# A planned transformer-block kernel on eight cores: gate pieces behind group 3's tiles, two more tile buffers, and new costs for GpSimd in the planner

## The reference

```python
mod_x = split(silu(c) @ w_ada + b_ada, 6)            # shift, scale, gate, twice
h   = layer_norm(x) * (1 + scale0) + shift0
q, k, v, u, vb, ga, gb = split(h @ w_in)
ya  = window_attention(rope(q), rope(k), v, kc, vc, sink)   # +-128 tokens and all context keys
yb  = gelu(u) * (w_s @ LN(gelu(vb)) + b_s)                  # per chunk of 128 tokens
mix = (sigmoid(ga) * (ya @ w_a) + sigmoid(gb) * (yb @ w_b)) @ w_out
x1  = post_norm(x, gate0 * mix)
h2  = layer_norm(x1) * (1 + scale1) + shift1
out = post_norm(x1, gate1 * ((silu(h2 @ w_g) * (h2 @ w_u)) @ w_d))
```

## Time and profile before

| | us |
|---|---|
| median of 3 runs | 981.92 |
| lowest and highest | 981.34, 982.61 |
| the profiled execution, its own time | 983.19 |
| its span from first to last instruction (core 4) | 981.4 |
| spans of the eight cores | 975.6 to 981.4 |
| PE busy / DVE / ACT / POOL | 897.0 / 624.9 / 321.6 / 275.3 |

### The profile page before, as it was taken

The page is one execution under the profiler, slowest core; times in us unless marked ns, Lnnn a source line. Parts: engine busy times, 40 slices in busy tenths (PEclk is TensorE's granted clock), DMA queues, the critical chain, the costliest instruction groups (busy, mean ns, idle before and its releaser), DMA issues.

```text
span 981.4 us, 15835 instructions; the slowest of 8 cores (975.6 to 981.4 us)
## 1 busy us (share of the span) xinstructions
PE 897.0 (91%) x5589; PEld 445.7 (45%) x5589; DVE 624.9 (64%) x1130; ACT 321.6 (33%) x497; POOL 275.3 (28%) x234
## 2 busy tenths in 40 slices
PE   1299697898999999999999999999999999999992
PEld 1245444344555444444444444444444444444761
DVE  5336687756655566776687575566556674666667
ACT  1336675546877243334435101110111001111101
POOL 6024164465464223323311630210202011000004
PEclk9999798989999999999999999999999999999997
DMA  8997621449972500027322580403304020111112
GB/s 211 195 196 179 166 87 44 108 55 167 146 106 68 172 1 1 1 86 112 106 40 75 159 196 1 86 6 81 82 4 86 1 43 1 43 64 43 44 65 86
DMA packets 30236, 83.91 MB, mean 86 GB/s; under 512 B 2896, under 2 KB 3152, under 8 KB 28496
## 3 DMA queue, kind: packets, MB, share of 16 engines
q0 software_dynamic: 18064, 34.54, 23.0%
q1 hardware_dynamic: 12096, 48.37, 14.2%
HBM read 109.05 MB, written 8.39 MB: 120 GB/s over the span
## 4 chain that ended last, share of the span: by engine, by line
PE 84%; DMA 6%; DVE 4%; issue 2%; ACT 1%; POOL 1%; SPq 0%; DVEq 0%; POOLq 0%; ACTq 0%
PE psum L1169 31%; PE psum L1195 15%; PE psum L1007 11%; PE psum L1058 6%; PE psum L1024 6%; DMA arena<-wqk 4%; PE psum L664 3%; PE psum L720 3%; PE psum L891 2%; PE psum L927 2%; PE psum L751 2%; DMA arena<-bsbc 1%; DVE arena L493 1%; PE psum L1093 1%; ACT arena L897 1%
## 5 line engine op out<-in xcount | busy, mean ns | idle before, releaser
L1169 PE MATMUL psum<-arena 128*128 128x512 bf16 (+1 forms) x1536 | 316.0, 361 | 0.0
L1169 PEld LDWEIGHTS psum<-arena 128*128 128x128 bf16 x1536 | 150.2, 98 | 154.1
L1175 ACT ACTIVATE arena<-psum 128x512 f32<-128x512 f32 (+1 forms) x96 | 53.9, 562 | 372.3 <-PE psum L1169 372.3
L1195 PE MATMUL psum<-arena 128*128 128x512 bf16 x704 | 163.0, 379 | 0.0
L1209 DVE TENSOR_TENSOR arena<-arena,psum 128x512 f32<-128x512 f32 x224 | 140.5, 680 | 29.8 <-PE psum L1195 29.7
L1178 DVE TENSOR_TENSOR arena<-psum,arena 128x512 bf16<-128x512 f32 (+1 forms) x96 | 62.0, 646 | 127.2 <-PE psum L1169 124.8
L500 POOL TENSOR_TENSOR arena<-arena 128x1 f32<-128x1 f32 (+1 forms) x74 | 47.9, 648 | 298.5 <-DVE arena L498 290.1
L1007 PE MATMUL psum<-arena 128*128 128x512 bf16 x512 | 117.5, 379 | 0.0
L493 DVE BATCH_NORM_STATS2 arena<-arena 128x6 f32<-128x512 f32 x152 | 98.3, 684 | 12.6 <-ACT arena L761 3.2
L1195 PEld LDWEIGHTS psum<-arena 128*128 128x128 bf16 x704 | 68.6, 98 | 82.2 <-issue 1.7
L897 ACT ACTIVATE arena<-psum 128x1024 bf16<-128x1024 f32 (+1 forms) x100 | 80.5, 852 | 25.1 <-PE psum L891 24.1
(11 more groups left out here) (97 smaller groups left out, 897.0 us busy)
## 6 DMA issues: line engine op xcount, KB each, us to landing
arena<-xh SPq DMA_DIRECT2D x34, 512.0 KB, 8.6
arena<-wada POOLq DMA_DIRECT2D x24, 512.0 KB, 17.4
arena<-wff POOLq DMA_DIRECT2D x11, 1024.0 KB, 10.3
arena<-wff SPq DMA_DIRECT2D x11, 1024.0 KB, 7.5
out<-arena SPq DMA_DIRECT2D x16, 512.0 KB, 2.6
arena<-wc POOLq DMA_DIRECT2D x8, 768.0 KB, 19.2
arena<-wout SPq DMA_DIRECT2D x8, 512.0 KB, 4.6
arena<-rope SPq DMA_DIRECT2D x4, 512.0 KB, 12.0
```

Of the source, the lines that this page charges most:

```text
L1169: ins = e.matmul(bank(ps)[:, 0:n], lhsT=w1v[r][:, k, lo:lo + 128], rhs=h2(k), start=(k == 0), stop=(k == 7))
L1175: s = P.op('act', prio - 150, act_cost(n), lambda e: e.activation(out=sgv(), in_=bank(pg)[:, 0:n], func=AF.Silu), after=[a], takes=[sg], g ...
L1195: ins = e.matmul(bank(ps), lhsT=actv[(r, fi, t)], rhs=w2v[r][:, fi, h * 512:(h + 1) * 512], start=(n == 0), stop=(n == 2 * len(rounds) - 1))
```

## The change

1. The gate pieces 8 to 11 take only spots 0 and 1 of `a4` (they had 0, 1, 6 and 7), and wait for the second tile of group 3 (`ld_x3[1]`) where they waited for the load of the v weights.
2. Group 3's tiles of x get two more buffers, spots 7 and 8 of `xr`, at qg + 24 KB and + 28 KB, ahead of 0 to 3 in their list.
3. The q, k and u work of group 3 no longer waits for the gate matmuls (`ada_mid`).
4. The planner counts 1.2 us instead of 0.12 us from the end of a POOL operation to what waits for it, and has other costs for five kinds of operation on POOL and DVE.

```diff
-    LAG = {'pe': 0.24, 'act': 0.10, 'dve': 0.10, 'pool': 0.12, 'sp': 0.1}
+    LAG = {'pe': 0.24, 'act': 0.10, 'dve': 0.10, 'pool': 1.2, 'sp': 0.1}
...
-    o_xr = [o_wo + 4 * KB * i for i in range(4)] + [L['qg'] + 8 * KB, L['qg'] + 12 * KB, L['vn'] + 4 * KB]
+    o_xr = [o_wo + 4 * KB * i for i in range(4)] + [L['qg'] + 8 * KB, L['qg'] + 12 * KB, L['vn'] + 4 * KB,
+                                               L['qg'] + 24 * KB, L['qg'] + 28 * KB]
...
     def norm_group(name, srcs, prio, after, engs=('act', 'act'), room=(0, 1, 2, 3)):
+        lds = []
         for i in (0, 2):
-            norm_pair(name, i, srcs[i:i + 2], prio + 0.1 * i, engs, after, room)
+            lds += norm_pair(name, i, srcs[i:i + 2], prio + 0.1 * i, engs, after, room)
...
+        return lds
...
-            res.append(P.op('pool', prio - 40, (hi - lo) / 512.0 * 1.1 + 0.2, lambda e, dst=dst, lo=lo, hi=hi: e.tensor_tensor(
+            res.append(P.op('pool', prio - 40, (hi - lo) / 512.0 * 1.3 + 0.2, lambda e, dst=dst, lo=lo, hi=hi: e.tensor_tensor(
...
-            t_vn[j] = P.op(me, prio + i - 20, 0.75 if me == 'dve' else 1.3, lambda e, gvs=gvs, j=j: e.tensor_tensor(
+            t_vn[j] = P.op(me, prio + i - 20, 0.9 if me == 'dve' else 1.5, lambda e, gvs=gvs, j=j: e.tensor_tensor(
...
-    norm_group('3', [xh[(13 + i) * 128:(14 + i) * 128, :] for i in range(4)], 64, [ld_wu[1]])
+    ld_x3 = norm_group('3', [xh[(13 + i) * 128:(14 + i) * 128, :] for i in range(4)], 64, [ld_wu[1]], room=(7, 8, 0, 1, 2, 3))
...
-        ada(8 + n, [(2, 2 * n), (2, 2 * n + 1)], 30 + n, (0, 1, 6, 7), after=[ld_wvvb])
-    ada_mid = ada_last[8:]
+        ada(8 + n, [(2, 2 * n), (2, 2 * n + 1)], 30 + n, (0, 1), after=[ld_x3[1]])
...
-    proj_qk(3, 108, ada_mid)
-    proj_u(3, 110, ada_mid)
+    proj_qk(3, 108)
+    proj_u(3, 110)
...
-                ex = P.op(me, prio + n * 0.1, 1.0 if me == 'dve' else 2.1, lambda e, ptv=ptv, mi=mi: e.tensor_tensor(
+                ex = P.op(me, prio + n * 0.1, 1.1 if me == 'dve' else 2.2, lambda e, ptv=ptv, mi=mi: e.tensor_tensor(
...
-        t_yb[j] = P.op('dve', prio + 0.9, 0.8, lambda e: e.tensor_tensor(
+        t_yb[j] = P.op('dve', prio + 0.9, 0.98, lambda e: e.tensor_tensor(
```

## The result

| | before | after |
|---|---|---|
| median of 4 runs each, us | 982.26 | 972.03 |
| lowest and highest | 981.34, 984.46 | 971.27, 973.53 |
| profiled execution, own time / span | 983.19 / 981.4 (core 4) | 973.53 / 972.0 (core 3) |
| ratio after to before, 95% interval | | 0.9889, 0.9875 to 0.9903 |

The change takes 10.9 us off by the ratio (1.1% of 984, the median of the kernel before in the later runs; between 9.5 and 12.3). The forecast was 974.6 us, between 964 and 985. In some executions, of the kernel before and of most experiments, the four cores of one die ran at a lower mean clock (0.80 to 0.81 where the kernel before took 1146 us), and all ratios leave those out.

What follows compares the result with a forecast made beforehand. PE was taken to lose time from 96 to 330 us and in the tail. Terms -6.3 + 1.0 - 2.0 + 0 = -7.3 us gave 975.9 us from 983.19, corrected by 1.27 to 974.6; range 964 to 985.

Steps and rivals of the forecast that it cites:

- What bounds the kernel: 96 to 330 us, where norms, projections and attention overlap, and 17.4 us behind the last matmul.
- term C: 130 to 250 us: the planner's new lag and costs close some of PE's idling, -2.0 us, between -12 and +8.
- Term A: 96 to 119 us: gate loads behind group 3's second tile end DVE's waits and a half-clock V tile, -6.3 us.
- The V tile: PE's tile at half clock from 106.27 to 110.69 us, 4.4 us, was to take 2.2 us, saving 2.2.
- Term B: PE or POOL's queue waiting at gate pieces, about 98 to 125 us: +1.0 us, between 0 and +10.6.
- The rival of the gates: Slower by the gates: 98 to 125 us, POOL's queue or PE stands at a gate piece; 986.2 us, chance 0.10.
- Term D: The tail behind the last matmul, where the last tile's statistics are delayed: 0 us, between -2 and +2.
- The collision rule: At 187.74 us DVE's two-SBUF-input operation stands until POOL pauses; flat cost and lag cannot place it; without term C 976.6 us.
- The lock's price as a rival for the slow side: Slower by collisions: DVE stands behind POOL, up to 3.6 us per L965; four more on PE's path, 986 us, chance 0.08.
- the two slow rivals: PE or POOL's queue held at gates, 98 to 125 us (986.2 us, 0.10); DVE standing behind POOL (986 us, 0.08).

Runs made afterwards that it cites:

- Traffic in an unchanged order: Kernel before, same order, each of four gate pieces moving only 128 of 2048 columns: ratio 0.9951, 4.8 us off, 3.5 by the medians.
- the gates alone: Parts 1 to 3 of the change on the kernel before, with its old lag and costs: ratio 0.9926, median 978.81 us against 984.07.
- the short masks: Kernel before, same order, POOL's 20 mask products (L906) on 128 of 1024 columns: 9.6 us off (7.5 to 11.8).
- the step to 0.20: Kernel before with the planner's lag behind POOL at 0.20 us instead of 0.12: ratio 0.9936, 6.3 us off.

## Why the prediction was right

The sign came out, and the time within the range: 974.6 forecast, 972.03 measured; a gain of 7.3 us forecast, 10.9 measured. Part of that is luck: a step of 0.08 us in one lag moved the kernel before by 6.3 us, nearly the whole forecast gain, and the prediction's causes hold only in part. Point by point:

- **What bounds the kernel** held. The gain lies between 96 and 330 us; the stretch from 52 us back and the tail gave nothing. Most of it lies in the waits from 130 to 250 us, on which the prediction put only its small term C.
- **Term A, -6.3 us for the gates.** The part measured 7.3 alone (5.3 by the medians), 5.7 on average over four settings. The landings went as forecast in kind: bsbc 7.0 us (forecast within 5), group 3's tiles from 93.67 us (92), the first gates at 104.00 us (98.5; the tile landed some 5 us later than my sum from the lone rate had it). What failed is the mechanism's share and its place. Traffic in an unchanged order costs 3.5 to 4.8 us where I had 6.3, which the interval (2.0 to 7.7) does not exclude. The V tile I gave 2.2 us still ran at half clock, for PE was idle before it just as long (2.81 us for 2.56). And with the gates alone the halo's k matmuls hardly moved, while later stretches gained.
- **Term B, +1.0 us**: no cost is seen. PE waits for no gate from 96 to 250 us, and POOL's holds of 1.90, 5.72 and 2.61 us have nothing urgent behind them. The rival of the gates had the holds right and their price wrong.
- **Term C, -2.0 us for the planner's numbers**: 3.6 us (10.9 less 7.3), with intervals wide enough for nothing to 7. Half of its ceiling is 12.9 us, (16.5 + 9.3) / 2, and not 12. The step that was wrong is calling it a margin. Beside gates and new costs the lag brings nothing (12.4 without it, 10.9 with it); what brings something there is the costs, and in the old setting every other order tried. The lag took 8.5 us alone, which was outside what I expected of it.
- **Term D, 0**: +0.6 us.
- **The collision rule.** The trace's sign of it was right, and the short masks show it: 7.2 us of DVE time in 16 instructions are due to POOL. Its conclusion, that term C would be a matter of luck, is borne out for the kernel before by the step to 0.20. The lock's price as a rival for the slow side did not come, since the new order has fewer: 16 L967 take 16.1 us in all after, 21.3 before. That fits the Trainium skill ("SBUF — State Buffer", "Who interferes with whom"), which has DVE with two SBUF inputs and GpSimd's reads exclude each other; the runs show the stall, and not by which port.

Of the profile's signs I had named, four failed although the forecast held: PE was to be busy above 18 us from 96 to 119, and had 15.12; its clock was to be above 0.9, and was 0.70; bsbc was to land in 5 us, and took 7.0; and POOL's queue was not to wait at the gates, and stood 10.2 us in three waits. The range has a slip of its own: the two slow rivals, 0.18 together, are priced at 986, above the 985 that it gives only 0.1 to exceed.

What stays open: why the gates and the lag, both strong alone, give no more together. Their traces differ on every engine, and no run here isolates one wait. Nor does a run part the three edits of the gates part: the later pieces, the two buffers and the dropped wait were always changed together.

## What to carry to other kernels

In a kernel whose order comes from a greedy planner, a change of a planner's number is a new draw over every engine: run a neighbour value or two before crediting the number (0.12 to 0.20 was worth 6.3 us here, and 0.12 to 1.5 no more than 2.1 us with the gates part and the new costs). Loads that are needed late go behind those needed at once, even where nobody waits for them by name: here that traffic cost some 4 us. And a vector operation whose duration varies, here from 0.68 to 4.30 us, may be standing behind GpSimd; shortening GpSimd's mask products was worth 9.6 us, nearly as much as the whole change.

## What the runs showed of the hardware that I had not expected

In the profiled execution after, cores 2 and 3 had a granted clock of 0.81 from 555 to 565 us, and of about 0.90 on average in the 5 us on either side, while PE was busy all the time; the other six had 1.00. The spans of the two cores are 1.6 to 5.7 us longer than those of the others in that execution. Windows of core 3 and of core 4 (stretch, PE busy, clock, DMA share, GB/s):

```profile
555.00:560.00 5.00, 5.00 (x21) 0.81 1.07 206
580.00:600.00 20.00, 20.00 (x94) 1.00 0.01 3
```

```profile
555.00:560.00 5.00, 5.00 (x25) 1.00 1.02 288
```

0.81 is neither of the two levels, 1.2 and 2.4 GHz. From 540 to 580 us core 3 made 175 matmuls where core 5 made 187; 12 at 0.214 us (40 us by 187) are 2.6 us. The Trainium skill ("TensorE: Matmul & The Clock Gate", "Seeing it yourself") tells of a peak-current limiter at 13/16, that is 0.8125, which takes a whole die while the load lasts. The number agrees; in this execution it took two cores of a die for under 20 us, with all eight at dense matmuls for 600 us. That the limiter is the cause is not shown.

Also new to me: an instruction on one or two elements per partition on DVE (L516, before) took up to 3.74 us, 0.16 at the median. The longest ran from 230.81 to 234.55 us, while POOL worked without a pause until 234.53 us. All L516 (min, median, max in ns), then POOL's timeline:

```profile
L516 DVE SCALAR_TENSOR_TENSOR arena<-arena x43: 134/159/3744, 27.1 to 965.7; 128x1 f32<-128x1 f32 x35, 128x2 f32<-128x2 f32 x8
```

```profile
230.14 1.08 POOL L500 TENSOR_TENSOR arena<-arena 128x1 f32<-128x1 f32 x2
231.19 1.26 POOL L768 TENSOR_TENSOR arena<-arena 128x512 bf16<-128x512 f32 x1
232.42 2.11 POOL L906 TENSOR_TENSOR arena<-arena 128x1024 bf16<-128x1024 bf16 x1
```

With POOL's masks short, in the same order, the longest L516 is 1.66 us. So it seems to be the stall of L965: DVE stands through several POOL instructions, however small its own is.
